# One layer pair of a hybrid decoder: the order of work in the SSD scans, in the turn to the output projection and at the entry of the FFN

## The chip, the cores and the metric

The kernel runs on one core of a Trainium2 chip. The metric is the device time of one execution in microseconds (us). TensorE is called PE here, VectorE DVE, ScalarE ACT, GpSimd POOL, and SyncE SP; SP issues nearly all DMAs.

## What is computed

The reference is a decoder trunk in float32 with 1024 tokens of width 1024 and two layers. Layer 0 is windowed attention beside a pooling mixer, then a SwiGLU FFN. Layer 1, where the change works, is a Mamba-2 SSD mixer and a second FFN:

```python
h = rmsnorm(x, mix_norm_w[1])
proj = h @ w_in                      # z (2048), xbc (3072), dt (32 heads)
xbc = silu(causal_depthwise_conv(xbc))
y = ssd_chunked(xs, dt, A, B, C) + xs * D      # 8 chunks of 128 tokens, 4 groups of 8 heads
y = y * silu(z)
y = y * rsqrt(mean(y * y over the group's 512 channels) + eps) * norm_w
x = x + y @ w_out                    # 2048 x 1024
h = rmsnorm(x, ffn_norm_w[1]); x = x + (silu(h @ w_gate) * (h @ w_up)) @ w_down
out = rmsnorm(x, final_norm_w)
```

In a chunk the scan computes C·B, masks it with the decay between tokens, multiplies it with x·dt (the diagonal part), adds C times the state before the chunk (the offset part), and updates the state.

## The kernel before

Each engine has a program of its own, written out by hand, and waits on semaphores; the order inside an engine is the order of the code. All products are three matmuls in a reduced float format: a value v is split into `hi` (rounded) and `lo` (v - hi, "the rest"), and hi·hi, lo·hi and hi·lo are added. So every operand needs an ACT instruction for `hi` and a DVE or POOL instruction for `lo`. The large products (both FFNs, the conv columns, the output projection) are done with seven instead of eight block products, M1 to M7, whose operands are sums and differences of the blocks (S1 to S4 are those of the left operand, T1 to T4 those of the FFN's input).

**Scans** (1181 to 1503 us of the trace). Four groups g of eight chunks c. Per chunk PE does `token_major` of the *next* chunk (C·B and transposes, line 2864 to 2871), the state product (L2957), the offset product (L2964), the diagonal product (L2974), and then half blocks of the z columns by `z_half` (L2228 to 2230), 12 matmuls each, 16 per group; `Z_AFTER_CHUNK` says which stand behind which chunk. ACT makes the decays (`mdec`, L2166 and L2171) and silu of z (`silu_z`). DVE masks the decays (`masked_decay`, L3835), reads the products back (`token_major`, L3768 to 3777: causal mask, B transposed, x·dt), updates the state (L3876) and writes y (L3884 to 3894). POOL scales x·dt for the state (`xds`, L1426) and the old state (L1429).

Around this run three side jobs, each of one group behind or ahead. (1) The z weights of a group are four pieces of 128x1024; SP loads them into two raw buffers, ACT makes hi (`next_hi`), POOL lo (L1143, one instruction a piece). (2) A group's y is finished in two halves of 512 tokens, h = 0 and 1, half number n = 2g + h: `gated` (times silu z, L3791), squares on ACT (L2121), their sum over four blocks on POOL (`square_sum`, L1405, three additions), a sum over partitions on PE (`square_sums`, L2883), root on ACT (L2128), reciprocal on DVE (L3796), then `root_row` on SP: the row is stored to DRAM and loaded back spread over all partitions (L939, L945). Then `row_normed` multiplies (L3802) and `mix` makes S1 to S4 (L3821). (3) SP stores the blocks to DRAM (`store_block`, L954, `gated_y`) for the projection, and loads the conv rows of the next group (`load_bc`, L885, `load_xrows`, L890) into buffers that the group before last has left.

SP works through all of that in one queue. `load_decay` (L933), first in every chunk, waits for a diagonal product, and everything behind it waits too.

**Turn and projection.** The output projection has 56 slices, (j, p): j is the block product in the order M1, M2, M5, M6, M4, M7, M3, p = 0 to 7 the 256 rows of y that it reads; p = 6 and 7 are the last group's. `OUT_SEQ` is their order, `o_places` their buffers, a ring of five behind four early ones. SP loads a slice (`load_out`, L983 and L986), ACT splits hi (`out_hi`, L2135 and L2138), DVE makes sums (`out_sum`) and the weights' rest (`out_low`, L3747), POOL the rest of y (`out_lo`, L1397), PE multiplies (`out_slice`, L2905, L2909, L2913; for p = 7 through `mm3`, L2228 to 2230) into four banks, and DVE adds the four tiles of a finished j to x (`add_result`, L3761). `out_loads` is SP's order for this part; the residual x comes back by `load_x_back`.

**Entry of the second FFN.** While the last slices (M3) run, the finished tiles of x (tt = 0 to 3 need M7, 4 to 7 need M3) are squared on ACT, normed on DVE (`make`, L3044), turned on PE (`second_T`, L2251), split on ACT and DVE (`lo`, L3101; `tail_...`, L3120 to 3157), and the first products of the FFN (L2525) wait for them: M6 for the rests of T2 (L3151).

## Time and profile before

| | us |
|---|---|
| median of 3 runs | 2369.83 (2365.24 to 2371.79) |
| the profiled execution | 2368.59 |
| its span, first to last instruction | 2366.9 |
| mean granted clock of PE | 0.982 |

The page gives busy time per engine, the chain of work that ended last, and groups of instructions. PE is busy for 96% of the span, DVE for 60%, ACT for 48%, POOL for 58%; 84% of the chain that ended last is PE. A wait is the idle time of an engine before an instruction, put down to what released it. The granted clock is PE's clock as a share of 2.4 GHz; 0.5 is its lower level, 1.2 GHz.

### The profile page before, as it was taken

The page shows a single profiled execution, that of the slowest core. Times are in us where ns is not written, and L with a number is a line of the kernel's source. Part 1 is how long each engine was busy: PE and PEld are TensorE (multiplying, and loading weights), DVE is VectorE, ACT ScalarE, POOL GpSimd, SP SyncE. Part 2 cuts the span into 40 slices and gives each one's busy share as a digit, 9 for nine tenths or more (in the row PEclk, how much of TensorE's full clock was granted, in tenths as well). Part 3 has the DMA queues.
Part 4 walks back from the last instruction along what each step waited for, and adds up shares of the span by engine and source line. Part 5 has one row for each costly group of instructions (what it writes and reads, how often), then busy time and mean ns, then how long its engine had stood idle before and what let it go on. Part 6 is the DMA issues. An engine that isn't in the chain of part 4 may idle for free.

```text
span 2366.9 us, 29286 instructions
## 1 busy us (share of the span) xinstructions
PE 2267.5 (96%) x10602; PEld 1841.8 (78%) x10602; DVE 1425.3 (60%) x1828; ACT 1146.5 (48%) x2101; POOL 1373.0 (58%) x992
## 2 busy tenths in 40 slices
PE   8999999999999999999999889779979999999998
PEld 6876888888888878888777667558768888888887
DVE  7366754333346888745578778658873424335787
ACT  4056643333334447555588767424643333333445
POOL 3234288777765654877344434235568777774654
PEclk9999999999999999999999989889999999999999
DMA  5110233232339653333444534476323233227844
GB/s 158 54 27 19 107 99 119 85 116 85 116 111 329 206 163 116 107 107 117 137 134 134 179 133 143 165 251 187 126 73 121 98 116 116 85 98 248 268 150 157
DMA packets 193787, 317.16 MB, mean 134 GB/s; under 512 B 21696, under 2 KB 106604, under 8 KB 191084
## 3 DMA queue, kind: packets, MB, share of 16 engines
q1 hardware_dynamic: 191212, 307.55, 38.6%
q10 hardware_dynamic: 2432, 7.73, 0.8%
q8 instruction: 86, 1.41, 0.2%
q14 instruction: 57, 0.47, 0.1%
HBM read 230.68 MB, written 84.56 MB: 133 GB/s over the span
## 4 chain that ended last, share of the span: by engine, by line
PE 84%; DVE 7%; DMA 3%; issue 2%; POOL 2%; SPq 1%; ACT 1%; DVEq 0%; ACTq 0%; POOLq 0%
PE ps L2525 42%; PE ps L2228 5%; PE ps L2230 5%; PE ps L2229 5%; PE ps L2617 5%; PE ps L2621 5%; PE ps L2613 5%; PE ps L2909 1%; PE ps L2913 1%; PE ps L2905 1%; PE ps L2251 1%; PE ps L2974 1%; PE ps L2694 1%; DMA bc_rows<-conv_rows 1%; PE ps L2957 1%
## 5 line engine op out<-in xcount | busy, mean ns | idle before, releaser
L1274 POOL TENSOR_TENSOR s_lo<-s_val,s_hi 128x512 fp32r<-128x512 f32 x154 | 236.1, 1539 | 197.3 <-ACT s_hi L1863 196.7
L3279 DVE TENSOR_TENSOR xres<-ps,xres 128x512 f32<-128x512 f32 x132 | 90.6, 688 | 407.5 <-PE ps L2525 407.5
L1172 POOL TENSOR_TENSOR p_lo<-p_val,p_hi 128x512 fp32r<-128x512 f32 x176 | 240.1, 1374 | 48.8 <-ACT p_hi L1616 43.3
L1616 ACT ACTIVATE p_hi<-p_val 128x512 fp32r<-128x512 f32 x176 | 111.0, 632 | 310.8 <-POOL p_val L1202 310.8
L1143 POOL TENSOR_TENSOR w_lo<-w_raw,w_hi 128x1024 fp32r<-128x1024 f32 x34 | 81.5, 2401 | 195.4 <-ACT w_hi L1471 108.7
L2525 PE MATMUL ps<-xn_hi,p_hi 128*128 128x512 f32 x704 | 190.8, 393 | 1.9 <-ACT xres L1765 1.3
L2525 PE MATMUL ps<-xn_lo,p_hi 128*128 128x512 f32 x704 | 188.8, 390 | 1.4 <-DVE xn_lo L3145 1.4
L2525 PE MATMUL ps<-xn_hi,p_lo 128*128 128x512 f32 x704 | 188.2, 389 | 0.0
L1863 ACT ACTIVATE s_hi<-s_val 128x512 fp32r<-128x512 f32 x154 | 96.9, 629 | 149.1 <-DMA d_val<-in_w_down 86.9
L2228 PE MATMUL ps<-xn_hi,w_hi 128*128 128x512 f32 x400 | 162.1, 405 | 0.0
L2229 PE MATMUL ps<-xn_lo,w_hi 128*128 128x512 f32 x400 | 157.2, 393 | 0.0
L2230 PE MATMUL ps<-xn_hi,w_lo 128*128 128x512 f32 x400 | 156.7, 392 | 0.0
L2525 PEld LDWEIGHTS ps<-xn_hi,p_hi 128*128 128x128 f32 x704 | 132.6, 189 | 30.2 <-ACT p_hi L1616 3.1
L2525 PEld LDWEIGHTS ps<-xn_lo,p_hi 128*128 128x128 f32 x704 | 132.7, 189 | 29.6 <-DVE xn_lo L3145 1.8
L2525 PEld LDWEIGHTS ps<-xn_hi,p_lo 128*128 128x128 f32 x704 | 132.1, 188 | 27.6
L2617 PE MATMUL ps<-d_lo,s_hi 128*128 128x512 f32 x560 | 151.4, 390 | 2.1 <-DVE d_lo L3331 1.9
L1397 POOL TENSOR_TENSOR os_lo<-os_val,os_hi 128x512 fp32r<-128x512 f32 x56 | 89.7, 1608 | 106.9 <-ACT os_hi L2135 106.7
L2613 PE MATMUL ps<-d_hi,s_hi 128*128 128x512 f32 x560 | 151.1, 390 | 0.0
L2621 PE MATMUL ps<-d_hi,s_lo 128*128 128x512 f32 x560 | 150.8, 389 | 0.0
L3331 DVE TENSOR_TENSOR d_lo<-rows_v,d_hi 128x512 fp32r<-128x512 f32 x108 | 127.2, 1181 | 20.9 <-ACT d_hi L1866 20.9
L1765 ACT ACTIVATE xres<-ps 128x512 f32<-128x512 f32 x132 | 77.9, 592 | 119.7 <-PE ps L2525 119.7
L2617 PEld LDWEIGHTS ps<-d_lo,s_hi 128*128 128x128 f32 x560 | 104.7, 188 | 26.1 <-DVE d_lo L3331 4.6
(385 smaller groups left out, 5680.0 us busy)
## 6 DMA issues: line engine op xcount, KB each, us to landing
s_val<-hidden SPq DMA_DIRECT2D x154, 256.0 KB, 2.9
hidden<-xres SPq DMA_DIRECT2D x20, 1792.0 KB, 6.5
wv_g<-in_w_gate SPq DMA_DIRECT2D x22, 1024.0 KB, 5.2
wv_u<-in_w_up SPq DMA_DIRECT2D x20, 1024.0 KB, 5.2
d_val<-in_w_down SPq DMA_DIRECT2D x70, 256.0 KB, 4.0
rows_v<-in_w_down SPq DMA_DIRECT2D x64, 256.0 KB, 3.7
mdec<-decay_sums SPq DMA_DIRECT2D x32, 512.0 KB, 3.9
os_val<-gated_y SPq DMA_DIRECT2D x56, 256.0 KB, 2.8
```

The costliest lines, as they stand in the source:

```text
L1172: pool.tensor_tensor(p_lo[n][:, :, :], src, f(p_hi[n][:, :, :]), ALU.subtract).then_inc(p_lo_done, 1)
L1274: pool.tensor_tensor(s_lo[i][:, :], s_val[i][:, :], f(s_hi[i][:, :]), ALU.subtract)\
L1616: act.activation(p_hi[n][:, :, :], src, ACT.Copy).then_inc(p_hi_done, 1)
L1863: act.activation(s_hi[i][:, :], s_val[i][:, :], ACT.Copy).then_inc(s_hi_done, 1)
L2228: pe.matmul(dst, l_hi, r_hi, start=first, stop=False, skip_group_check=reopened)
L2229: pe.matmul(dst, l_hi, r_lo, start=False, stop=False, skip_group_check=reopened)
L2230: return pe.matmul(dst, l_lo, r_hi, start=False, stop=last, skip_group_check=reopened)
L2525: ins = pe.matmul(bank, l_[:, k, :], r_[:, k, :], start=first and k == 0, stop=last and k == H2 - 1, skip_group_check=reopened)
L2613: pe.matmul(banks[t_], s_hi[i][:, t_ * P:(t_ + 1) * P], d_hi[i][:, :], start=p == 0, stop=False)
L2617: pe.matmul(banks[t_], s_hi[i][:, t_ * P:(t_ + 1) * P], d_lo[i][:, :], start=False, stop=False)
L2621: pe.matmul(banks[t_], s_lo[i][:, t_ * P:(t_ + 1) * P], d_hi[i][:, :], start=False, stop=False)\
L3331: dve.tensor_tensor(d_lo[i][:, :], down_operand(DOWN[j], p, i), f(d_hi[i][:, :]), ALU.subtract).then_inc(d_lo_done, 1)
```

## The change

Eight things are moved or exchanged; nothing is computed otherwise.

1. SP: in group g the rows of half 0 for group g + 1 are loaded at chunks 4 and 5 (before: 6), those of half 1 at chunk 0 of their own group (before: 7 of the one before); stores and weight pieces are spread over the chunks; the first root row of a group is sent at chunk 7 of that group (before: 0 of the next), the second at chunk 3 (before: 4).
2. DVE: norm, gating, mixes and reciprocals stand between `masked_decay(c)` and `token_major(c + 1)`, not behind it, and one or two chunks earlier.
3. The sums of squares go from POOL (three in a row) to DVE (`square_adds`, two and one); PE's sum over partitions comes at chunks 2 and 6 (before: 3 and 7), ahead of the z half blocks.
4. POOL makes the rests of the weight pieces in halves (`half_lo`), the first one ahead of `xds`.
5. ACT: squares, roots, hi of the pieces and silu change their chunks.
6. Projection: two more M2 slices stand before (0, 6) and (0, 7); slices 2, 4 and 5 are loaded at chunk 6, slice 3 at chunk 7; the order of SP in `out_loads` is new; buffers of slices 2 and 3 are other ones.
7. The rests of y for slices 0 to 15 are made by DVE (`out_s_low`), for the others by POOL as before; M1's additions come as 4 and 12 behind slices 14 and 15 (before: 8, and 4 per slice).
8. Entry of the FFN: M7's additions and squares go to p = 0 to 3, turnings to p = 1, 3, 4, 5, turning 5 ahead of the second product, and the tail's order on DVE and ACT is new.

```diff
-        OUT_SEQ = ([(0, p) for p in range(6)] + [(1, p) for p in range(3)] + [(0, p) for p in (6, 7)] ...
+        OUT_SEQ = ([(0, p) for p in range(6)] + [(1, p) for p in range(5)] + [(0, p) for p in (6, 7)] ...
...
-        SILU_AFTER_CHUNK = [{1: (0, 1), 4: (2, 3, 4)}] + [{2: (0, 1), 4: (2, 3), 6: (4, 5)}] * (G - 1)
-        NEXT_PIECE = {6: 0, 7: 1}
-        LATE_PIECE = {0: 2, 1: 3}
+        SILU_AFTER_CHUNK = [{1: (0, 1), 3: (2, 3), 5: (4,), 7: (5,)}]
+        SILU_AFTER_CHUNK += [{3: (0, 1), 5: (2, 3), 7: (4, 5)}] * (G - 2) + [{3: (0, 1), 5: (2, 3), 6: (4,), 7: (5,)}]
+        PIECE_HI = [{0: 2, 1: 3}] + [{0: 1, 1: 2, 2: 3}] * (G - 1)
+        LO_AHEAD = [{1: (2, 0), 2: (3, 0)}] + [{0: (0, 1), 1: (1, 0), 2: (2, 0), 3: (3, 0), 4: (3, 1)}] * (G - 1)
+        LO_BEHIND = [{1: (2, 1), 2: (3, 1)}] + [{1: (1, 1), 2: (2, 1)}] * (G - 1)
+        S_LO_DVE = 16
...
@@ SP, ssd_group, q = g - 1
                     if c == 0 and g:
-                        root_row(2 * g - 2)
+                        sp.wait_ge(y_stored, 16 * 14 * q)
+                        load_xrows(g, 1)
+                        sp.wait_ge(y_normed, BG * (2 * q + 1))
+                        store_blocks(q, "M4")
+                        load_piece(g, 3)
                     if c == 2 and g:
-                        first_stores(g - 1)
+                        sp.wait_ge(mix_ready, 8 * q + 2)
+                        store_blocks(q, "M5")
+                        if not last:
+                            load_piece(g + 1, 0)
+                    if c == 3 and g:
+                        sp.wait_ge(y_stored, 16 * (14 * q + 4))
+                        root_row(2 * q + 1)
-                    if c == 4 and g:
-                        sp.wait_ge(y_stored, 16 * (14 * (g - 1) + 4))
-                        root_row(2 * g - 1)
+                    if c == 4:
+                        if g and not last:
+                            load_bc(g + 1, 0)
+                        if g:
+                            sp.wait_ge(y_normed, BG * 2 * g)
+                            store_blocks(q, "M1")
+                        if g and not last:
+                            load_piece(g + 1, 1)
+                    if c == 5:
+                        if g:
+                            sp.wait_ge(mix_ready, 8 * q + 4)
...
+                        if not last:
+                            load_xrows(g + 1, 0)
+                        if g:
+                            store_blocks(q, "M7")
-                    if c == 6:
-                        if g:
-                            sp.wait_ge(y_normed, BG * 2 * g)
-                            store_blocks(g - 1, "M1", "M2")
-                            sp.wait_ge(mix_ready, 8 * (g - 1) + 4)
-                            store_blocks(g - 1, "M7")
...
-                        if not last:
-                            load_xrows(g + 1, 0)
-                            load_bc(g + 1, 0)
+                    if c == 6 and last:
+                        load_out(2)
+                        load_out(4)
+                        load_out(5)
                     if c == 7:
+                        root_row(2 * g)
+                        if not last:
+                            load_bc(g + 1, 1)
+                            load_piece(g + 1, 2)
...
+                        if last:
+                            load_out(3)
@@ SP, out_loads
+                load_out(6)
+                load_out(7)
+                load_out(8)
+                sp.wait_ge(y_stored, 16 * 14 * q)
+                root_row(2 * q + 1)
+                sp.wait_ge(y_normed, BG * (2 * q + 1))
+                store_blocks(q, "M4")
+                load_out(9)
+                sp.wait_ge(mix_ready, 8 * q + 2)
+                store_blocks(q, "M5")
+                load_out(10)
+                sp.wait_ge(y_normed, BG * (2 * q + 1) + 2)
+                store_blocks(q, "M1")
+                sp.wait_ge(y_stored, 16 * (14 * q + 6))
+                load_out(11)
...
+                sp.wait_ge(mix_ready, 8 * G)
+                store_blocks(q, "M6", "M3")
+                sp.wait_ge(y_stored, 16 * 14 * G)
+                load_out(14)
@@ POOL
+            def half_lo(piece, half):
+                cols = slice(half * BANK, (half + 1) * BANK)
+                pool.wait_ge(hi_done, piece.count(1))
+                ins = pool.tensor_tensor(w_lo[piece.slot][:, cols], raw[piece.raw][:, cols], f(w_hi[piece.slot][:, cols]),
+                                         ALU.subtract)
+                if half:
+                    ins.then_inc(lo_done, 1)
@@ DVE, ssd_group
                     masked_decay(c)
+                    if c == 0 and g:
+                        for b in range(BG):
+                            row_normed(g - 1, b, 0)
+                    if c == 1 and g:
+                        gated(g - 1, 1)
+                    if c == 2 and g:
+                        square_adds(2 * g - 1)
+                        mixes(g - 1, "S1")
+                    if c == 3 and g:
+                        reciprocal_rms(2 * g - 1)
+                    if c == 4 and g:
+                        for b in H1_ORDER:
+                            row_normed(g - 1, b, 1)
+                    if c == 5:
+                        if g:
+                            mixes(g - 1, "S3")
+                        gated(g, 0)
+                    if c == 6:
+                        square_adds(2 * g)
+                        if g:
+                            mixes(g - 1, "S2")
+                    if c == 7:
+                        reciprocal_rms(2 * g)
+                        if g:
+                            mixes(g - 1, "S4")
                     if k + 1 < NT * G:
                         token_major(k + 1)
-                    if c == 0 and g:
-                        gated(g - 1, 1)
-                        reciprocal_rms(2 * g - 2)
...
+            def square_adds(n):
+                dve.wait_ge(sq_ready, BG * (n + 1))
+                dve.tensor_tensor(sq[0][:, :], sq[0][:, :], sq[1][:, :], ALU.add).then_inc(sq_added, 1)
+                dve.tensor_tensor(sq[2][:, :], sq[2][:, :], sq[3][:, :], ALU.add).then_inc(sq_added, 1)
+                dve.wait_ge(sq_added, 2 * (n + 1))
+                dve.tensor_tensor(sq[0][:, :], sq[0][:, :], sq[2][:, :], ALU.add).then_inc(sq_summed, 1)
@@ DVE, entry of the FFN, s_ from 10
+                        if s_ < S_LO_DVE:
+                            out_s_low(s_)
-                        if (j, p) == (1, 7):
-                            quota, limit = 8, "M1"
-                        elif j >= 2 and p in (0, 1):
-                            quota, limit = (4, "M1") if j == 2 else (0, "M1")
+                        if (j, p) in ((1, 6), (1, 7)):
+                            quota, limit = 4 if p == 6 else 12, "M1"
...
+                    make(6)
+                    tail(0)
+                    make(7)
+                    tail(1)
+                    tail(2)
...
```

## Rows read from the trace of the kernel before

**Rows 1.** The page, busy time of each engine over the span.

```profile
PE 2267.5 (96%) x10602; PEld 1841.8 (78%) x10602; DVE 1425.3 (60%) x1828; ACT 1146.5 (48%) x2101; POOL 1373.0 (58%) x992
```

**Rows 2.** Windows by stage: length, then busy us (x instructions) of each engine.

```profile
1181.70:1503.50 321.80, 291.14 (x1762) 231.96 (x1761) 256.12 (x441) 240.53 (x478) 122.23 (x87) 0.95 0.42 141
1503.50:1594.00 90.50, 59.78 (x213) 45.16 (x212) 51.53 (x73) 25.26 (x44) 35.29 (x22) 0.79 0.67 235
1594.00:1676.20 82.20, 82.20 (x363) 67.72 (x363) 67.82 (x84) 38.65 (x71) 42.32 (x28) 1.00 0.57 179
1676.20:1745.30 69.10, 52.53 (x246) 41.84 (x245) 58.80 (x70) 44.36 (x86) 34.58 (x22) 0.94 0.27 95
```

**Rows 3.** Waits of PE in the scans: us in total, times, longest.

```profile
PE ps L2864 <- DMA bc_rows<-conv_rows: 20.2, 3, 7.4
PE ps L2974 <- DVE mdec L3835: 8.7, 5, 2.1
```

**Rows 4.** Timeline of PE (start us, us, instruction): three chunk starts.

```profile
1446.46 0.38 PE L2864 MATMUL ps<-bc_rows 128*128 128x128 f32 x2
...
1455.67 0.38 PE L2864 MATMUL ps<-bc_rows 128*128 128x128 f32 x2
...
1466.11 0.38 PE L2864 MATMUL ps<-bc_rows 128*128 128x128 f32 x2
```

**Rows 5.** Timeline of SP's queue: the stores and loads before a group change.

```profile
1403.47 1.79 SPq L954 DMA_DIRECT2D gated_y<-yx  x4
...
1406.92 0.68 SPq L885 DMA_DIRECT2D bc_rows<-conv_rows  x1
```

**Rows 6.** Timeline of POOL: three sums of squares.

```profile
1349.92 4.41 POOL L1405 TENSOR_TENSOR sq<-sq,sq 128x512 f32<-128x512 f32 x3
```

**Rows 7.** Timeline of DVE: masking under those sums, and without them.

```profile
1353.11 3.22 DVE L3835 TENSOR_TENSOR mdec<-mdec,cbm 128x512 f32<-128x512 f32 x2
...
1371.04 1.29 DVE L3835 TENSOR_TENSOR mdec<-mdec,cbm 128x512 f32<-128x512 f32 x2
```

**Rows 8.** Groups of DVE, 1181.7:1413.6: count, busy us, mean ns, idle before.

```profile
L3791 DVE TENSOR_TENSOR yx<-zs,yx 128x512 f32<-128x512 f32 x19 | 17.6, 983 | 0.0
L3802 DVE SCALAR_TENSOR_TENSOR yx<-yx,gconst,rr 128x512 f32<-128x512 f32 x16 | 16.7, 1106 | 0.0
...
L3768 DVE TENSOR_TENSOR cbm<-ps,tri 128x128 f32<-128x128 f32 x22 | 6.3, 285 | 28.6 <-PE ps L2866 22.6 <-PE ps L2864 6.0
```

**Rows 9.** Waits of PE, 1503.5 to 1594 us.

```profile
PE ps L2909 <- DVE od_lo L3747: 18.0, 2, 9.5
PE ps L2905 <- DVE xres L3761: 7.4, 3, 3.1
```

**Rows 10.** Timeline of DVE: gating of the last half group.

```profile
1507.94 2.50 DVE L3791 TENSOR_TENSOR yx<-zs,yx 128x512 f32<-128x512 f32 x4
```

**Rows 11.** Timeline of ACT: root of its sum of squares.

```profile
1524.36 0.36 ACT L2128 ACTIVATE rinv<-ps,eps 4x128 f32<-4x128 f32 x1
```

**Rows 12.** Chain of waits after the scan: start us, us, what.

```profile
1516.18 6.82 DMA rr_rows<-rinv
1523.02 3.93 DMA rr<-rr_rows
...
1534.11 4.41 DMA gated_y<-mix_S
1538.54 1.16 DMA rr_rows<-rinv
1539.71 3.63 DMA rr<-rr_rows
```

**Rows 13.** DMA from 1500 to 1600 us.

```profile
DMA packets 12332, 22.98 MB, mean 230 GB/s; under 512 B 1260, under 2 KB 1268, under 8 KB 12327
```

**Rows 14.** Waits of PE, 1676.2 to 1745.3 us.

```profile
PE ps L2525 <- DVE comb_lo L3151: 7.2, 1, 7.2
PE ps L2251 <- DVE xn_lo L3135: 4.1, 1, 4.1
```

More of the change, by code:

```diff
@@ L1065, in out_loads @@
+                        if last:
+                            load_out(3)
             def out_loads(load_gate):
[L1066 to L1068 removed]
+                q = G - 1
                 load_out(6)
                 load_out(7)
[L1071 to L1075 removed]
@@ L1099, in out_loads @@
+                load_out(15)
+                load_x_back(3)
+                load_x_back(7)
+                for s_ in range(16, OUTS):
                     load_out(s_)
@@ L1421, in factor @@
                         return gconst[:, g, first + c * HG:first + (c + 1) * HG].unsqueeze(2).to_broadcast([P, HG, PH])
+                    if c in LO_AHEAD[g]:
+                        b, half = LO_AHEAD[g][c]
+                        pool.wait_ge(cb_full, NT * g + c + 1)
+                        if (g, c) == (0, 1):
+                            pool.wait_ge(product_full, q_order.count(0, NQ - 1, "M4g"))
+                        half_lo(piece(b), half)
+                    if c == NT - 1 and g < G - 1:
+                        pool.wait_ge(cb_full, NT * g + c + 1)
+                        half_lo(in_group(g + 1)(0), 0)
                     if c < NT - 1:
@@ L1703, in second_entry @@
                 def second_entry():
-                    for s_ in range(5, OUTS):
+                    for s_ in range(6, OUTS):
                         j, p = OUT_SEQ[s_]
@@ L1714, in second_entry @@
                             half_square(p + 2, 0)
+                        if j == 6 and p < 4:
+                            for tt in ((0,), (1,), (2,), (3,))[p]:
+                                act.wait_ge(out_added, o_add_order.count(0, "M7", tt, 0, 1))
+                                square(tt, junk[:, :])
                         if (j, p) == (6, 2):
@@ L2182, in ssd_group @@
                         row_silu(row_at(NQ - 1, "g", 2))
-                    if c == 1 and g:
-                        squares(2 * g - 1)
-                    if c == 5:
-                        squares(2 * g)
-                    if c in LATE_PIECE:
-                        next_hi(g, LATE_PIECE[c])
-                    if c in NEXT_PIECE and not last:
-                        next_hi(g + 1, NEXT_PIECE[c])
+                    if c == 3 and g:
+                        root(2 * g - 1)
+                    if c == 7:
+                        root(2 * g)
                     if c >= 6 and last:
@@ L2934, in ssd_group @@
             def ssd_group(g):
-                last = g == G - 1
-                SUMS_AT = (3, 6) if last else (3, 7)
                 if g == 0:
@@ L2976, in ssd_group @@
                     ins.then_inc(ydiag_full, 1)
-                    if c in SUMS_AT:
-                        *first, final = Z_AFTER_CHUNK[g][c]
-                        for i in first:
-                            z_half(g, i)
-                        if c == 3 and g:
-                            square_sums(2 * g - 1)
-                        elif c == (6 if last else 7):
-                            square_sums(2 * g)
-                        z_half(g, final)
-                    else:
-                        for i in Z_AFTER_CHUNK[g][c]:
-                            z_half(g, i)
+                    if c == 2 and g:
+                        square_sums(2 * g - 1)
+                    elif c == 6:
+                        square_sums(2 * g)
+                    for i in Z_AFTER_CHUNK[g][c]:
+                        z_half(g, i)
                 t.add("chunk", NT)
@@ L3216, in second_entry @@
                     taken = 0
-                    for s_ in range(6, OUTS):
+                    for s_ in range(10, OUTS):
                         j, p = OUT_SEQ[s_]
@@ L3250, in second_entry, with tail @@
                         add_result("M3", t_, 4, 1)
-                    for q in range(4, NT):
-                        make(q)
-                    for i in range(4):
+                    make(4)
+                    make(5)
+                    def tail(i):
                         tail_t1(i)
@@ L3791, in gated, with mixes @@
                     dve.tensor_tensor(half_of(g, b, h), z[:, :], half_of(g, b, h), ALU.mult).then_inc(z_gated, 1)
+            def square_adds(n):
[4 more added lines that the diff above has]
+                dve.tensor_tensor(sq[0][:, :], sq[0][:, :], sq[2][:, :], ALU.add).then_inc(sq_summed, 1)
+            def mixes(g, *names):
+                for name in names:
+                    for i in range(2):
+                        mix(g, name, i)
             def reciprocal_rms(n):
```

269 lines of the change are left out of this document (123 added, 146 removed), and 2 rows, old and new, of the table Z_AFTER_CHUNK.

## The prediction

> **What bounds the kernel now.** I read the busy times first [rows 1]: PE works for 96% of the span, so only time in which PE waits, or multiplies at the lower of its two clock levels (1.2 instead of 2.4 GHz), can be given back. Then the windows [rows 2], cut where the diff works: the scans, the turn from scans to projection, the steady projection, the entry of the second FFN. The reader is to compare length and PE busy. The projection from 1594 us is full (82.2 of 82.2, clock 1.00) and can give nothing. In the scans PE is idle for 321.8 - 291.1 = 30.7 us, in the turn for 90.5 - 59.8 = 30.7 us, at the entry for 69.1 - 52.5 = 16.6 us, and in all three the granted clock falls below 1 (0.95, 0.79, 0.94): each longer wait is followed by some matmuls at half rate. Third the waits of PE in each stretch [rows 3, 9, 14], last the chain of waits behind the scans [rows 12].
>
> What would each stretch need at full rate? A slice of the projection is 12 matmuls: 82.2 / 363 x 12 = 2.72 us [rows 2]. A half block of z (one `z_half`) has the same 12. A chunk with two of them takes 1455.67 - 1446.46 = 9.21 us, so its own work is 9.21 - 5.44 = 3.77; one with the sum of squares takes 10.44, so that costs 1.23 [rows 4].
> - Scans: 59 half blocks (160.5) + 31 chunks (116.9) + 7 sums (8.6); at the ends of groups six products are missing, about a quarter of 3.77 each (-5.7, an estimate). Together 280.3 of 321.8: 41.5 us are lost, 30.7 idle and 10.8 at half clock.
> - Turn, first slice at 1503.5 to the start of the 18th at 1594: 17 x 2.72 + 1.23 = 47.5 of 90.5, 43 lost.
> - Entry: 16.6 idle and at most (1 - 0.94) x 69.1 = 4.1 at half clock: 20 lost.
>
> So about 105 us are there to be had, and that is the ceiling.
>
> **The change part by part.**
>
> *Loads before a group change.* Now SP issues the next group's rows at chunk 6, behind four waits and eight stores (1403.47, then the load at 1406.92 [rows 5]); PE comes to the next group's first chunk before they land and waits 20.2 us in three places, up to 7.4 each [rows 3]. In the new order rows of half 0 go out at chunk 4 or 5, behind the norm of the second half (DVE, now chunk 4) and the S3 mixes (chunk 5). From chunk 5's product to the next group's first product PE has a chunk and two half blocks and more, some 12 us, against 7.4 plus the issue. All 20.2 goes, and with it its part of the 10.8. Half 1 is loaded at chunk 0 of its own group and needed at chunk 3 or 4, over 25 us later. SP now waits in one more place, for the round trip of the root at chunk 7 and chunk 3; behind it stand the decay load of the next chunk and a weight piece. That trip's first part took 1.16 to 6.82 us [rows 12]; decay loads have two chunks, 18 us. I cost it at nothing; without that cover it is up to 5 us per group, 15.
>
> *DVE: norm, gating and mixes ahead of `token_major`.* They stand now where DVE waits for PE anyway (the idle time ahead of L3768, 28.6 us over 22 chunks [rows 8]); before, they stood between `token_major` and the masking on which the next product waits, which gave PE's 8.7 us [rows 3]. The number of these instructions is unchanged. What is new on DVE are the square sums: 3 per half group, 7 in the scans, at 1.29 / 2 = 0.65 each [rows 7]: +13.7 us. What goes is POOL's version: 4.41 us for three [rows 6], under which DVE's masking took 3.22 instead of 1.29 [rows 7], so at least 1.93 x 7 = 13.5 us less on DVE. DVE stays near 256 us busy [rows 2], of 290 instead of 322: 88%. Chunks with the heavy extras (four norms or gates at 0.98 to 1.11 [rows 8], 4.4 us) fit PE's 9.2 only because light ones follow. I keep 10 of the 41.5 us as lost. Ends: none lost (gain 41.5); or 15 behind the queue above and 10 behind DVE (gain 16). I take 31.5, nearer the first, because the largest row (20.2) is a DMA that simply goes out 12 us earlier.
>
> *POOL: rests of weight pieces in halves.* Same arithmetic, one instruction more per piece, 12 to 14 in all, on an engine busy 122 of 322 us [rows 2]. A half goes ahead of `xds` instead of a whole after it; it can delay `xds` by half of what it did. Zero, between -2 and +3.
>
> *The turn.* Today the second and third of PE's waits, 18.0 us, are for DVE rests behind the norm [rows 9]. Their chain has two round trips of the root through memory in a row: 6.82 + 3.93, then a store of 4.41, then 1.16 + 3.63 [rows 12]. The first trip now happens inside chunk 7. Slices 2, 4 and 5 load at chunk 6, which removes the wait at the third slice. Two more slices of M2 (p = 3, 4) stand before the first that needs the last group's M1 block, slice 11. PE gets to it at 11 x 2.72 + 1.23 = 31 us after the scan. Its data: gating starts at +4.5, root 12 to 16 later (1507.94 to 1524.36, of which part was the wait for the first trip [rows 10, 11]), trip 4.8 to 10.8, two norms 2.2 [rows 8], store 4.4, load as long, hi and lo rest 2: +34 to +44, middle 39. So about 8 us of waiting stay at slice 11 (3 to 13). Slice 14 loads after all stores of the last group, and slice 16 needs the 16 additions of M1, which DVE now makes in one row behind slice 14 (0.65 each, 10 us beside 8 us of PE work): 3 us each. Sum lost 14 of 43, gain 29. Ends: 3 lost (gain 40), and gain 5 if the chain takes its long values at each step and every load waits behind it in SP's order. Low rests of slices 0 to 15 move to DVE: 16 x 0.65 = 10 us, in a stretch where DVE works 51.5 of 90.5 [rows 2]; hidden, except the two ahead of the square sums.
>
> *Entry of the FFN.* M7 is added tile by tile from p = 0, turnings and the tail go up. The 4.1 us ahead of turning 6 were DVE's rest of tile 0, which moves ahead of `make(7)`: 0.5 stays. The 7.2 us [rows 14] were eight T4 and T2-rest instructions behind everything else; with two DVE instructions taken out ahead of them and turning 5 a slice earlier, I keep 3. Against that ACT now waits once per slice for DVE's addition and DVE for ACT's split; the first four slices may lose 3 where they lost 3. Gain 8, between 1 and 13.
>
> **Sum.** 31.5 + 29 + 8 = 68.5 us. The profiled execution took 2368.6 (span 2366.9 and 1.7 around it), which gives 2300; the median of the runs is 2369.8, 1.2 higher, so I say 2301.
>
> **Rivals.**
> - *The turn stays late.* SP's queue and the DMA engines take over the wait: 22.98 MB went out in 100 us, at 230 GB/s [rows 13], and must now go in about 71. If the chain to slice 11 ends at +44 and the loads behind it bunch, the turn gives 10, the scans 28, the entry 6: 44 us, 2326. For it speaks that the root's first trip took 6.82 us just where loads were queued [rows 12]; against it, that the mean hides empty stretches.
>   The Trainium skill (DMA: Bandwidth & Descriptors, "Where 436 GB/s comes from") puts one core's share of the memory at about 358 GB/s. By that the 22.98 MB need 64 us: no bar to my 71, but a bar to the next rival, whose turn would leave 60. The trace's mean of 230 neither reaches nor contradicts it.
> - *Nearly all goes.* 38 in the scans, 38 in the turn, 12 at the entry: 88 us, 2282. For it: every wait named has its cause moved. Against: the chain to slice 11 is longer than the work before it even at middle values.
> - *Slower: DVE becomes the bound of the scans.* Place: groups 1 to 3, where the norm and gating now stand ahead of `token_major`, so that every microsecond DVE is late reaches the next chunk's states. If all 90 extra instructions and 48 maskings run at the slow 3.22 / 2 = 1.61 instead of some 0.8 [rows 7], DVE needs 138 x 0.8 = 110 us more, 366 in place of 256; the scans take 366 instead of 322, +44, the other two give back 37, together +7: 2377. It decides from 322 + 37 = 359 us of DVE in the scans, 11.2 a chunk (now 8.0). Against it: POOL has 30 us less to do, and that is what slows these instructions.
> - *It doesn't bring what it says*: the waits only change their names, 2345 to 2370.
>
> **How the numbers follow.** Forecast 0.52; turn stays late 0.27; nearly all goes 0.13; slower 0.03; names change 0.05, of which 0.02 within 0.3%. A change of under 0.3%, 7 us, can't be told from none. Faster 0.95, same 0.02, slower 0.03. Range: 2282 (nearly all) to 2332 (the late turn with 6 us of POOL's and SP's bounds on top). The forecast's own range is 2288 to 2314.
>
> **What would show it.** PE's wait at L2864 for conv_rows gone; waits on masking under 5 us; scans 285 to 296 us long; DVE busy there 250 to 262. One root trip after the last scan product; PE's longest wait in the turn between 3 and 13 us at the slice (0, 6), 17 slices in 57 to 66 us. Largest wait at the entry under 4. I am wrong in the sum if DVE's busy time in the scans passes 275, if a wait for decay sums or for `xds` appears at PE's chunk starts, or if slices 3 to 10 wait for loads.

## The result, and the profile after

The changed kernel takes 2337.58 us (median of 4 runs, 2335.96 to 2337.85), the kernel before beside it 2367.53: a ratio of 0.9871 (95% interval 0.9852 to 0.989). It is faster by 30 us. The forecast of 2301 was too low by 37, and the range, which ended at 2332, missed the time.

Page of the changed kernel, busy times; then its windows, cut at the same landmarks as [rows 2] (first product of the scans, first slice, 18th slice, product of slice (5, 7), M3g).

```profile
PE 2259.0 (97%) x10602; PEld 1837.1 (79%) x10602; DVE 1409.0 (60%) x1868; ACT 1152.3 (49%) x2106; POOL 1312.3 (56%) x966
```

```profile
1180.60:1479.84 299.24, 284.94 (x1762) 228.23 (x1761) 249.62 (x469) 245.84 (x482) 91.27 (x79) 0.98 0.47 154
1479.84:1556.49 76.65, 57.55 (x215) 44.67 (x214) 48.00 (x80) 23.98 (x42) 3.90 (x3) 0.84 0.78 269
1556.49:1638.10 81.61, 81.61 (x362) 67.57 (x360) 67.79 (x87) 39.73 (x72) 49.44 (x31) 1.00 0.57 181
1638.10:1713.74 75.64, 55.06 (x246) 42.79 (x244) 60.75 (x74) 45.12 (x88) 31.71 (x21) 0.89 0.24 87
```

Set against [rows 2], the scans lost 22.6 us (forecast 31.5), the turn 13.9 (forecast 29), the steady part 0.6, and the entry got 6.5 us *longer* (forecast 8 shorter). The span fell by 32.7; of what the four windows leave, 1.1 lies ahead of the scans and 1.1 behind the start of M3g. PE did the same work: what moved is idle time and half clock.

Waits of PE in the changed kernel (us in total, times, longest), in the scans, which answer to [rows 3]; in the turn, which answer to [rows 9]; and at the entry, which answer to [rows 14]:

```profile
PE ps L2913 <- DVE btok L3810: 6.4, 3, 3.0
PE ps L3002 <- DVE mdec L3890: 5.8, 4, 3.1
PE ps L2913 <- DVE cbm L3806: 1.3, 2, 1.0
```

```profile
PE ps L2935 <- ACT od_hi L2168: 11.4, 3, 4.8
PE ps L2259 <- DVE os_lo L3785: 5.6, 1, 5.6
PE ps L2935 <- DVE xres L3799: 1.4, 1, 1.4
```

```profile
PE ps L2556 <- ACT comb_hi L1686: 12.7, 1, 12.7
PE ps L2935 <- ACT od_hi L2168: 5.6, 3, 3.2
```

No line of the first list existed before except the masking. The wait for `conv_rows` (20.2 us) is gone; in its place PE waits at its sum over partitions (L2913, `square_sums`), which the change put one chunk earlier. In the turn the rests behind the norm (18.0 us) are gone, and slices 3, 13, 14 and 15 wait for their data. At the entry one wait of 12.7 us stands where 7.2 and 4.1 stood.

### The profile page after: what moved, and what is told of

The parts are those of the page before. It is cut to its first block, busy times and chain, and to the rows that moved or that the text cites. A ratio compares the mean times of both kernels' runs of the same rounds, so it can differ in the third digit from the quotient of the medians.

```text
span 2334.2 us, 29295 instructions
## 1 busy us (share of the span) xinstructions
PE 2259.0 (97%) x10602; PEld 1837.1 (79%) x10602; DVE 1409.0 (60%) x1868; ACT 1152.3 (49%) x2106; POOL 1312.3 (56%) x966
## 4 chain that ended last, share of the span: by engine, by line
PE 84%; DVE 7%; DMA 3%; ACT 2%; issue 2%; POOL 1%; SPq 1%; DVEq 0%; ACTq 0%; POOLq 0%
PE ps L2556 43%; PE ps L2259 5%; PE ps L2261 5%; PE ps L2260 5%; PE ps L2648 5%; PE ps L2652 5%; PE ps L2644 5%; PE ps L2939 1%; PE ps L2935 1%; PE ps L2943 1%; PE ps L2725 1%; PE ps L2282 1%; PE ps L3002 1%; DVE yx L3954 1%; DVE d_lo L3364 1%
## 5 line engine op out<-in xcount | busy, mean ns | idle before, releaser
L2556 PE MATMUL ps<-xn_hi,p_hi 128*128 128x512 f32 x704 | 189.9, 392 | 14.0 <-ACT comb_hi L1686 12.7
L2648 PE MATMUL ps<-d_lo,s_hi 128*128 128x512 f32 x560 | 151.4, 390 | 1.9 <-DVE d_lo L3364 1.7
L1430 POOL TENSOR_TENSOR os_lo<-os_val,os_hi 128x512 fp32r<-128x512 f32 x40 | 63.3, 1585 | 141.5 <-DVE os_lo L3785 85.9
L2652 PEld LDWEIGHTS ps<-d_hi,s_lo 128*128 128x128 f32 x560 | 105.1, 188 | 21.9
```

Source lines behind the costliest of these rows:

```text
L2556: ins = pe.matmul(bank, l_[:, k, :], r_[:, k, :], start=first and k == 0, stop=last and k == H2 - 1, skip_group_check=reopened)
L2648: pe.matmul(banks[t_], s_hi[i][:, t_ * P:(t_ + 1) * P], d_lo[i][:, :], start=False, stop=False)
L2652: pe.matmul(banks[t_], s_lo[i][:, t_ * P:(t_ + 1) * P], d_hi[i][:, :], start=False, stop=False)\
```

## Experiments

Each run was timed in five rounds beside the kernel before. "Against the change" compares the median with 2337.6; the ratio is to the kernel before.

| run | median us | ratio (95%) | against the change |
|---|---|---|---|
| e1 tail order | 2331.7 | 0.9840 (0.9826 to 0.9855) | -5.9 |
| e2 sums later | 2325.5 | 0.9817 (0.9803 to 0.9832) | -12.1 |
| e3 slice 3's load first | 2334.3 | 0.9853 (0.9836 to 0.9869) | -3.3 |
| e4 store order | 2329.5 | 0.9833 (0.9819 to 0.9848) | -8.1 |
| e5 additions early | 2334.2 | 0.9855 (0.9842 to 0.9869) | -3.4 |
| e6 norm later | 2334.6 | 0.9862 (0.9847 to 0.9877) | -3.0 |
| e7 kernel before, rows early | 2353.0 | 0.9944 (0.9932 to 0.9957) | (-14.2 against before) |
| e8 e1 to e5 together | 2313.8 | 0.9773 (0.9760 to 0.9787) | -23.8 |
| e9 turn ordered anew | 2310.1 | 0.9757 (0.9741 to 0.9774) | -27.4 |
| e10 e9 and e6 | 2305.5 | 0.9734 (0.9718 to 0.9750) | -32.0 |
| e11 e10, stores first | 2304.4 | 0.9734 (0.9719 to 0.9749) | -33.2 |

The intervals of e3, e5 and e6 overlap that of the change and that of e1 touches it, so there the traces carry the verdict. As a yardstick for stretches whose code is the same: in the changed kernel, e1, e3, e4 and e5 the scans took 299.1 to 300.4 us from the first diagonal product to the first slice, and in the changed kernel, e1, e2 and e6 turn and steady part took 166.5 to 168.3.

### The entry: e1

```
 tail_t1(3)
 tail_t2(3)
+tail_t3(3)
+tail_b22(3)
 tail_lo1(2)
 ...
     tail_lo2(i)
-tail_t3(3)
-tail_b22(3)
```

> The changed kernel with one edit: VectorE's last difference and rest of tile 7 (tail_t3(3), tail_b22(3)) stand right behind tail_t2(3) again, ahead of the four tail_t4/tail_lo2 pairs. The changed kernel takes 2337.6 us. Theory A (the 12.70 us wait of the first M5g product at 1705.72 is the wait for tile 7's PSUM banks, read last by those two operations at 1704.35 and 1704.95): they end near 1695.4, M5g starts near 1695.6, and its sixth wait partner, M6g's pass over the low parts, is late instead, since the four pairs still end near 1705.6: entry shorter by 6 to 8 us, time 2329 to 2332. Theory B (M5g waits for ScalarE's high parts, as the page's releaser says, which come no earlier): no gain, 2336 to 2339.

Timeline of VectorE in the changed kernel (start us, us, line), and the product that waits, on TensorE:

```profile
1701.01 1.75 DVE L3163 TENSOR_TENSOR t_val<-t_val,comb_val 128x512 f32<-128x512 f32 x1
1702.68 1.74 DVE L3174 TENSOR_TENSOR comb_lo<-comb_val,comb_hi 128x512 fp32r<-128x512 f32 x1
1704.35 0.68 DVE L3153 TENSOR_TENSOR comb_val<-ps,comb_val 128x512 f32<-128x512 f32 x1
1704.95 0.67 DVE L3158 TENSOR_TENSOR xn_lo<-ps,xn_hi 128x512 fp32r<-128x512 f32 x1
```

```profile
1705.72 2.04 PE L2556 MATMUL ps<-xn_hi,p_hi 128*128 128x512 f32 x4 [12.70 <-ACT comb_hi L1686]
```

Waits at the entry in e1:

```profile
PE ps L2556 <- DVE comb_lo L3174: 5.0, 1, 5.0
PE ps L2556 <- DVE xn_lo L3158: 2.4, 1, 2.4
```

The time fell by 5.9 us, at the edge of theory A (6 to 8). L3153 and L3158 are the last two readers of tile 7's PSUM banks; M5g opens a sum in them, through `turn_free(1, 7)`. With both back in their place the wait is 2.4 us, and now carries the name of the true releaser. The page had named ScalarE's high part: it was the last event before the start, not the cause. In e1 the product starts at 1695.76, before ScalarE's first such instruction (1698.39). M6g waits 5.0 us for the last T2 rest, where it waited 7.2 in the kernel before.

### The scans: e2, e6, e7

e2, TensorE, chunk 2 of scans 1 to 3:

```
-if c == 2 and g:
-    square_sums(2 * g - 1)
 for i in Z_AFTER_CHUNK[g][c]:
     z_half(g, i)
+    if c == 2 and g and i == 4:
+        square_sums(2 * g - 1)
```

> The changed kernel with one edit: TensorE takes the sum over partitions of the odd squares (square_sums(2g-1)) after the first of the two z halves of chunk 2 instead of ahead of both. Theory A (that sum waits 6.4 us in three scans for VectorE, which stands behind square_adds and the two S1 mixes before it frees the bank, and TensorE runs at half clock after each): the 5.5 us half covers the wait, 6 to 9 us less, time 2329 to 2332. Theory B (VectorE is what paces the scans and the wait only moves to the masking or to the root): less than 2 us, 2335.5 to 2338.

First what the sum waits for, in the changed kernel. VectorE's timeline, and TensorE's:

```profile
1341.23 0.68 DVE L3834 TENSOR_TENSOR sq<-sq,sq 128x512 f32<-128x512 f32 x1
1341.83 0.68 DVE L3835 TENSOR_TENSOR sq<-sq,sq 128x512 f32<-128x512 f32 x1
1342.55 1.64 DVE L3837 TENSOR_TENSOR sq<-sq,sq 128x512 f32<-128x512 f32 x1
1344.11 1.28 DVE L3876 TENSOR_TENSOR mix_S<-yx 128x512 f32<-128x512 f32 x2
1345.31 0.28 DVE L3806 TENSOR_TENSOR cbm<-ps,tri 128x128 f32<-128x128 f32 x1
1345.51 0.27 DVE L3810 COPY btok<-ps 128x128 f32<-128x128 f32 x1
```

```profile
1345.93 1.86 PE L2913 MATMUL ps<-sq,pick 128*4 128x128 f32 x8 [2.99 <-DVE btok L3810]
1347.73 0.80 PE L2259 MATMUL ps<-xn_hi,w_hi 128*128 128x512 f32 x1
1348.32 0.63 PE L2260 MATMUL ps<-xn_lo,w_hi 128*128 128x512 f32 x1
```

The squares' sum is ready at 1344.2, but it goes into the bank that `token_major(3)` has to free, and that stands on VectorE behind the three additions and the two mixes. TensorE had been idle since 1342.9: some 1.3 us of the wait are the additions, the other 1.7 the mixes and the reading of the bank. The eight small matmuls then take 1.86 us instead of 1.03, and the z half behind them starts slow too (0.6 to 0.8 us for each of its first matmuls instead of 0.39). Window of the scans in e2:

```profile
1181.23:1468.49 287.26, 279.89 (x1761) 223.80 (x1761) 249.22 (x469) 246.26 (x483) 92.53 (x79) 1.00 0.50 160
```

12.0 us less than 299.24: 6.9 of idle time and 5.1 of half clock (PE busy 284.94 to 279.89). Theory A, and more than it promised (6 to 9): its upper end left only 2.6 us for half clock beside the 6.4 of waiting.

e6, VectorE:

```
-if c == 0 and g: row_normed(g - 1, b, 0) for the four b
-if c == 1 and g: gated(g - 1, 1)
+if c == 1 and g: the four row_normed, then gated(g - 1, 1)
```

> The changed kernel with one edit on VectorE: the four norms of the first half stand behind the masking of chunk 1 instead of behind that of chunk 0. Theory A (the 5.8 us that TensorE waits for the masking come from the 4.43 us that VectorE waits, ahead of these norms, for the root's row): the waits of 3.08 and some 0.8 us go, 3 to 7 us less than 2337.6, 2330 to 2334.5. Theory B (SyncE waits for these norms before it goes on to a weight piece and the decay loads, on which ScalarE waits 28.6 us already): the later norms make these loads later and the wait comes back, 2336 to 2345.

Waits of VectorE and of ScalarE in the scans of the changed kernel, and waits of TensorE in e6 as its timeline shows them in scan 1:

```profile
DVE yx L3853 <- DMA rr<-rr_rows: 23.0, 6, 4.4
```

```profile
ACT eacs L2189 <- DMA mdec<-decay_sums: 24.5, 9, 5.4
```

```profile
1259.62 1.10 PE L3002 MATMUL ps<-mdec,xdt 128*64 128x128 f32 x16 [0.26 <-DVE mdec L3890]
1264.19 1.13 PE L2913 MATMUL ps<-sq,pick 128*4 128x128 f32 x8 [3.48 <-DVE btok L3810]
```

The scans are 1.7 us shorter (297.58 from first product to first slice, 1.5 below the shortest of the yardstick), the median 3.0, just outside theory A's range. The mask wait of 3.08 us in scan 1 became 0.26, but the sum's wait of 0.35 became 3.48. Theory A by direction, with most of its gain turned into the other wait. VectorE stands still for 23.0 us in six places until the root's row is back from memory, where it did so nowhere in the scans of the kernel before. Only a part of that reaches TensorE: all its waits for the masking are 5.8 us. ScalarE waits 24.5 us for decay sums (before: 7.4), which SyncE issues in the same queue; whether the trip causes these was not tried.

e7, the kernel before, SyncE:

```
+c == 4, g in (1, 2): load_bc(g + 1, 0)
+(g, c) == (0, 5): load_bc(1, 0); load_xrows(1, 0)
 c == 6: sp.wait_ge(y_normed, ...)
-        store_blocks(g - 1, "M1", "M2")
         sp.wait_ge(mix_ready, ...)
-        store_blocks(g - 1, "M7"); load_xrows(g + 1, 0); load_bc(g + 1, 0)
+        load_xrows(g + 1, 0); store_blocks(g - 1, "M1", "M2", "M7")
```

> The kernel before (2368.3 us) with one edit on SyncE: the next group's B and C rows of half 0 are loaded at chunk 4, its x rows at chunk 6 ahead of the six stores instead of behind them (both at chunk 5 in the first scan). VectorE and GpSimd work as before. Theory A (the scans' gain is the wait for these rows and nothing else of the change; x rows can go out only 3 us earlier in scans 1 and 2): the 20.2 us become 3 to 8, with their half clock 14 to 21 us less, 2347 to 2354: most of the 22.6 us that the scans gained. Theory B (half of the gain is VectorE's order and GpSimd's share taken off it): the wait moves to the masking or to xds, under 9 us less, over 2359.

Window of its scans, and the two waits that stay:

```profile
1181.00:1489.50 308.50, 288.38 (x1761) 229.69 (x1760) 256.93 (x441) 240.29 (x478) 122.17 (x87) 0.97 0.45 147
```

```profile
1313.46 0.79 PE L2866 MATMUL ps<-bc_rows 128*128 128x128 f32 x2 [4.57 <-DMA yx<-conv_rows]
...
1400.13 0.80 PE L2866 MATMUL ps<-bc_rows 128*128 128x128 f32 x2 [4.54 <-DMA yx<-conv_rows]
```

Earlier rows alone, with VectorE and GpSimd untouched, took 13.3 us off the scans [rows 2], for 11.1 us less of waiting (20.2 to 9.1): theory A by the time, with a little more wait left than its 3 to 8. By the same rate the 9.1 us that stay are worth about 11 (an estimate from these two figures), which makes some 24 in all, 1.6 more than the 22.6 that the scans gained. By that estimate everything else in the scans (VectorE's order, the squares moved off GpSimd, against the new wait) cost 1.6 net, and with e2's 12.0 for the wait it brought some 10 of its own. No run tried that part alone, so the 10 are not shown.

### The turn: e3, e4, e5

e3, SyncE, chunk 7 of the last scan:

```
+if last: sp.wait_ge(mix_ready, 8 * g); load_out(3)
 root_row(2 * g)
 ...
 store_blocks(q, "M3")
-if last: load_out(3)
```

> The changed kernel with one edit: SyncE issues the loads of output slice 3 ahead of the last root row's store, wait and load and of the M3 stores, 6 us earlier (near 1481 instead of 1486.8). Theory A (the turn is late by SyncE's order, in a chain: slice 3's wait of 4.84 us also holds ScalarE, behind it the last root, behind that all stores of the last scan and the loads of slices 13 to 15): the 4.84 us go and the later stores come 5 to 7 us earlier, 7 to 14 us less in all, time 2323 to 2331. Theory B (the transfers at 1530 to 1550, at some 400 GB/s, set the end of the turn whatever came before): the 4.84 us come back at slices 13 to 17, 0 to 3 us less, 2334.5 to 2338.

SyncE's queue in the changed kernel, from the root's row to slice 3's loads, and the slice on TensorE; then the reciprocal on VectorE that the root's row waits for, and SyncE's longest single wait between 1440 and 1482 us:

```profile
1480.77 0.33 SPq L946 DMA_DIRECT2D rr_rows<-rinv  x1
1485.45 0.32 SPq L952 DMA_DIRECT2D rr<-rr_rows  x1
1485.87 0.85 SPq L961 DMA_DIRECT2D gated_y<-mix_S  x2
1486.77 0.45 SPq L987 DMA_DIRECT2D os_val<-gated_y  x1
```

```profile
1494.11 2.04 PE L2935 MATMUL ps<-od_hi,os_hi 128*128 128x512 f32 x4 [4.84 <-ACT od_hi L2168]
```

```profile
1473.60 0.94 DVE L3847 RECIPROCAL rinv<-rinv 4x128 f32<-4x128 f32 x1 [1.55 <-ACT rinv L2158]
```

```profile
SPq L987 <- PE ps L2261: 11.6, 1, 11.6
```

The queue is late before the root's row already. `load_out(2)`, which the change puts at chunk 6, waits for the last z half block, and SyncE stands there for 11.6 us, until 1478.02. The reciprocal is done at 1474.54, but its row goes out at 1480.77, behind the six loads of slices 2, 4 and 5, and slice 3 behind the row's trip. What it would bring to send the row ahead of `load_out(2)` was not tried; e3 moves slice 3 alone.

In e3 that wait is gone. These are there, at slices 8, 10, 13 and 14; the last two stood before as well, with 2.60 and 3.95:

```profile
1504.91 1.20 PE L2940 MATMUL ps<-od_lo,os_hi 128*128 128x512 f32 x4 [1.10 <-DVE od_lo L3781]
1512.82 1.21 PE L2940 MATMUL ps<-od_lo,os_hi 128*128 128x512 f32 x4 [2.08 <-DVE od_lo L3781]
...
1524.58 1.25 PE L2936 MATMUL ps<-od_hi,os_hi 128*128 128x512 f32 x4 [3.45 <-ACT od_hi L2169]
1533.43 2.05 PE L2936 MATMUL ps<-od_hi,os_hi 128*128 128x512 f32 x4 [4.28 <-ACT od_hi L2169]
```

From the first slice to the first turning (all of turn and steady part) it takes 167.4 us, in the changed kernel 167.0: nothing gained in the turn; the 3.3 us of the median lie within the intervals. Theory B by the size. But the trace gives another reason than the transfers at 1530 to 1550: the root came 5.2 us earlier (its row is stored at 1493.55, not 1498.76), and then lost 3.1 of them, since the trip took 4.31 us behind the loads of slices 6 to 8 instead of 1.18. What comes last is the last scan's stores, and they came only 2.3 us earlier.

e4, SyncE:

```
 load_out(8)
+for tt in (4, 0, 5, 1): load_x_back(tt)
 ...
 store_blocks(q, "M2")
-load_x_back(0); load_x_back(4); ... store_blocks(q, "M7"); load_out(13)
-load_x_back(1); load_x_back(5); ... store_blocks(q, "M6", "M3")
-sp.wait_ge(y_stored, 16 * 14 * G); load_out(14); ... load_out(15); ...
+load_out(13); sp.wait_ge(y_stored, 16 * (14 * q + 8)); load_out(14); load_out(15)
+... store_blocks(q, "M7"); load_out(16); ... store_blocks(q, "M6", "M3")
+load_x_back(2); load_x_back(6); load_out(17); load_x_back(3); load_x_back(7)
+(the wait for all stores ahead of load_out(22))
```

> The changed kernel with SyncE's order in the turn changed: four of the eight 512 KB loads of parked rows are issued at 1491, in the idle stretch of the DMA engines, the loads of slices 14 and 15 wait for the M2 stores alone and are issued ahead of the M7, M6 and M3 stores, the wait for all stores stands ahead of slice 22. Theory A (slices 13 to 17 wait because their loads stand behind stores and parked rows that nobody needs yet): 3.95 us at slice 14, 5.59 at 15 and most of 2.60 at 13 go with their half clock, 8 to 13 us less, time 2324 to 2330. Theory B (bandwidth: the same bytes are to be moved before slice 18 at up to 400 GB/s): the waits move to slices 6 to 13 or 16 to 20, 0 to 3 us less, 2334.5 to 2338. Loads of the parked rows beside slices 6 to 8 and the last root's row could also cost up to 3 us.

Turn and steady part take 160.3 us instead of 167.0, the median falls by 8.1: theory A. The waits of 2.60 and 3.95 us at slices 13 and 14 are gone. Two rows show what then ends last:

```profile
1533.91 2.48 DVE L3801 TENSOR_TENSOR xres<-ps,rows_v 128x512 f32<-128x512 f32 x4 [6.91 <-DMA gated_y<-mix_S]
```

```profile
1538.26 0.80 PE L2261 MATMUL ps<-od_hi,os_hi 128*128 128x512 f32 x1 [7.60 <-DVE os_lo L3787]
```

The additions of M1 write `xres`, in which the mixes lie until they are stored, so they wait for the last scan's last stores; and slice 15's rests stand behind them on VectorE.

e5, VectorE:

```
-if s_ + 1 < OUTS: out_sum(s_ + 1)
+if s_ + 1 < OUTS and s_ != 15: out_sum(s_ + 1)
 out_low(s_); out_s_low(s_)
+if s_ == 15: four additions; out_sum(16)
-quota = 4 if p == 6 else 12
+quota = 8 if p == 6 else 4
```

> The changed kernel with one edit on VectorE: slice 15's two rests stand ahead of out_sum(16), and 8 instead of 4 of the 16 additions of M1 stand between slices 14 and 15, 4 ahead of out_sum(16) and 4 behind it. The changed kernel takes 2337.6 us. Theory A (the 5.59 us at slice 15 are VectorE's order: it waits until 1544.19 for slice 16's weights, though slice 15's high part is there at 1540.7, and the 12 additions in one row hold slice 16): slice 15 starts near 1542, slice 16 near 1549.5 instead of 1553.2, 3 to 5 us less, 2332.5 to 2335. Theory B (the stretch is paced by the transfers, and the additions need the parked rows, which land no earlier): 0 to 1.5 us less, 2336 to 2338.

```profile
1544.58 0.50 PE L2259 MATMUL ps<-od_hi,os_hi 128*128 128x512 f32 x1 [2.14 <-DVE os_lo L3790]
```

5.59 us became 2.14, turn and steady part 164.3, 2.2 below the shortest of the yardstick: theory A, at its lower end. (The first slice stands 2.1 us later in this trace than in that of the changed kernel, which the start times carry along.)

### Together: e8 to e11

> The changed kernel with the edits of the first four runs and that of the fifth together. Alone the first four gave 6, 12, 3 and 8 us against 2337.6. Theory A (each takes away a wait of its own): they add up, 29 us, and 3 of the fifth, 2303 to 2310. Theory B (the turn's edits work on the same wait, the last scan's stores, and the DMA engines at 400 GB/s bound them): only 18 of tail and sums and 6 to 8 of the turn, 2311 to 2315.

2313.8, theory B: the scans take 289.1 (e2: 287.3), the entry from its first turning to M6g's last pass 60.0 as in e1 (changed kernel 66.0), but turn and steady part 159.6, only 0.8 better than e4 alone. In e8:

```profile
1495.63 2.74 DVE L3861 SCALAR_TENSOR_TENSOR yx<-yx,gconst,rr 128x512 f32<-128x512 f32 x4 [6.90 <-DMA rr<-rr_rows]
...
1523.61 4.88 DVE L3807 TENSOR_TENSOR xres<-ps,rows_v 128x512 f32<-128x512 f32 x8 [6.67 <-DMA gated_y<-mix_S]
```

With slice 3 first, the root is ready at 1482.7, and its row (2 KB) now stands behind 2 MB of parked rows: store issued at 1484.25, load at 1492.04.

e9 is e8 with SyncE's order `load_out(7)`, `root_row(2q+1)`, `load_out(8)`, the stores, parked rows in pairs, and all stores ahead of slices 14 and 15; VectorE has 8 additions behind slice 13 and slice 15's rests ahead of the other 8. e10 adds e6.

> The kernel of the run before (all five edits, 2313.8 us), with the turn's order changed once more. There the four early parked rows stood ahead of the last root's row, whose trip took 7.8 us, and the additions of M1 waited 6.67 us for the last stores, with slice 15's rests behind them (9.34 us of TensorE at slice 15). Now the root's row goes out behind the loads of slice 7, the parked rows behind it in pairs; the M7, M6 and M3 stores go out as soon as their mixes are done, ahead of the loads of slices 14 and 15; on VectorE 8 additions stand behind slice 13, and slice 15's rests ahead of the other 8. Theory A (the order of SyncE's queue and of VectorE sets the turn): the last stores land near 1514 instead of 1523, slice 16 starts near 1527 instead of 1535, 6 to 10 us less, 2304 to 2308. Theory B (the DMA engines bound it: 21 MB at 400 GB/s are 53 us of the 65 from the first slice to the 18th): 0 to 4 us less, 2310 to 2314.

> The kernel of the run beside it, and VectorE's four norms of the first half behind the masking of chunk 1. Alone that gave 3.0 us, with the waits for the masking (5.8 to 2.9 us) partly turned into waits of the sum over partitions; here that sum is covered by a z half. Theory A: both gains stand, 3 to 6 us less than the run beside it. Theory B (VectorE has no more room in chunks 1 and 2, and the later sum delays the root): 0 to 1.5 us less or slower.

e9 gave 3.6 us against e8 (4.4 in turn and steady part, 155.1), in theory B's range by the size: the M7, M6 and M3 stores go out from 1507.1, not at 1512.5 and 1515.6. But slice 10 waits 4.57 us: its rest stands on VectorE behind the S2 mix, which waits for the M1 stores, and those stand behind 1 MB of parked rows. What holds it up there is again an order, not the rate of the transfers. e10 gave 4.6 more, theory A (scans 286.5 instead of 289.6, PE busy in them 280.16; the turn and steady part are 3.5 shorter as well, though the edit is in the scans). Windows of e10, scans, then turn and steady part together:

```profile
1181.12:1467.65 286.53, 280.16 (x1762) 223.85 (x1761) 249.33 (x469) 246.40 (x483) 89.49 (x79) 1.00 0.50 161
1467.65:1619.26 151.61, 142.06 (x611) 114.92 (x609) 129.12 (x173) 67.16 (x122) 50.74 (x34) 0.98 0.71 239
```

> The kernel of the last run (2305.5 us) with one edit: two 512 KB loads of parked rows that stood ahead of the last scan's M1 stores stand behind them. Theory A (the stores that the last mixes and slice 11 wait for are held up by what is queued ahead of them: at some 400 GB/s 1 MB is 2.6 us): VectorE's wait of 3.95 us for the M1 stores and TensorE's of 3.93 us at slice 11 shrink by 2 to 3 us, the last stores go out that much earlier, 1.5 to 3.5 us less, 2302 to 2304. Theory B (the same bytes have to go before the additions anyway, and the engines are at 400 GB/s from here on): the 2.6 us come back at slice 14, no change, 2304.5 to 2306.5.

e11 took 2304.4, turn and steady part 151.4: no change that can be told from none, so theory B, though the time lies between the two ranges. VectorE's wait for the M1 stores fell from 4.0 to 1.4 us and TensorE's of 3.93 to 1.87 (it is slice 10's, not slice 11's, as I had written), and waits of 1.57 and 0.64 us came up at slices 11 and 15, not at slice 14 as theory B had it. e10 and e11, with one ratio of 0.9734, are 32 to 33 us faster than the changed kernel and come within 5 us of the time I had forecast for it.

## Why the prediction missed

Of the signs I had named, these came: the wait for `conv_rows` gone, DVE busy 249.6 us (said: 250 to 262). These did not: masking under 5 us (5.8), scans 285 to 296 us (299.2), 17 slices in 57 to 66 us (76.7), the turn's longest wait at the slice (0, 6) (none there; 5.6 at (1, 7)), one root trip after the last scan product (two, with stores at 1480.77 and 1498.76, the last product having ended near 1479.9), largest wait at the entry under 4 (12.7). And slice 3 waited for its load, which I had named as what would make the sum wrong.

- **What bounds it: right.** The full-rate need of the scans, 280.3 us of PE, is what e2 and e10 show (279.89, 280.16 busy, clock 1.00).
- **Loads before a group change: right.** All 20.2 us went; e7 shows that the loads' place alone takes 11.1 of them away, at 1.2 us for each us of wait.
- **DVE ahead of `token_major`: the step that failed in the scans.** Busy time came as said (249.6, forecast 250 to 262). But I weighed VectorE by its busy time and took only the masking for exposed (5.8 us, said: under 5 to 10). Moved ahead of `token_major`, the additions and mixes also stand ahead of the bank that PE's sum takes. PE waited 7.7 us there, and e2 took 12.0 away, half clock included, where I had no term. Lost in the scans 18.9, kept 10; with e2's one edit 7.0 are lost. The root's trip, which "I cost ... at nothing" with a view to SyncE's queue alone, costs something by another way: VectorE waits 23.0 us for it, the longest time (4.43 us) shortly ahead of the 3.08 us masking wait, and e6, which puts the norms later, gains 1.7 us in the scans.
- **POOL in halves: right**, 0.6 us of waits for `xds`.
- **The turn: failed by 15 us.** The two root trips [rows 12] no longer stand in a row, but "the first trip now happens inside chunk 7" failed: both come after the last scan product, the first 6.2 us later than its row was ready, since the loads of slices 2, 4 and 5 ahead of it waited for the last z half block. The 8 us at slice 11 did not come: its rest began at +37 us (1517.1; my middle was +39), but PE got there at +39, not +31, held at slice 3 by 4.84 us and by the slow matmuls behind it. Slice 11's wait is hidden by that, not gone. I had taken slices 2 to 10 as loaded. Slice 3's load stood behind `root_row(2g)`: of what stands behind that trip in SyncE's queue I had named decay loads and a piece, and left slice 3 out. For slice 14, which loads after all stores, and for slice 16 with the additions I gave 3 us each; slices 13 to 15 took 12.1 idle, slice 16 another 1.4. The last stores were issued from 1520.93 and slice 14's load at 1530.54, 9.6 us later, and parked rows stood ahead of the loads of slices 13 and 15. I had priced the additions by VectorE's time and not by what they can wait for, the stores out of `xres`; in e4 that is 6.91 us. Idle was 19.1 us, half clock 10.0 (76.65 - 57.55, and 57.55 - 47.5).
- **The entry: wrong sign.** I counted "two DVE instructions taken out ahead of" the T2 rests and did not ask who waited for those two. They free M5g's banks: 12.7 us of waiting where I had kept 3, and 5.9 us less in e1. With them back the entry is as long as before, so the 8 us did not come either: M6g still waits 5.0, and the slices of the last product wait 2.24 and 3.25 us for ScalarE's high parts, which stand there among squares that wait for VectorE's additions tile by tile. I had given the slices 3 us, as before.
- **Rivals.** *The turn stays late* was nearest (2326, for turn 10, scans 28, entry 6): stores and loads bunched in SyncE's order are what e4 and e9 show. But its other condition, a chain to slice 11 that ends at +44, did not come (+37). It had a chance of 0.27; its time is 12 us short of the measured one, for which its entry term, 12.5 us off, suffices.

## What to carry to other kernels

Before moving work forward on an in-order engine, list for every instruction that it passes who waits for that one, buffers that it frees included, and put a matmul that needs another engine's latest results between pieces of independent work. A root or a flag that travels through memory belongs ahead of the bulk transfers in its queue, and ahead of whatever waits for a buffer there: the store of the same 2 KB row took 1.2 us when the loads issued before it had landed, 4.3 us behind the loads of three slices (e3) and 7.8 us behind 2 MB (e8). Price TensorE's waits together with the slow matmuls behind them: in the turn 10.0 us stood beside 19.1 of idle time, in e2 5.1 went with 6.9, in e7 2.8 with 10.5.

## What the runs showed of the hardware

DMA of the changed kernel from 1530 to 1550 us, 40 slices of half a microsecond:

```profile
GB/s 8 0 4 131 315 402 238 115 262 369 385 385 336 365 373 258 274 324 406 385 397 397 410 410 402 397 410 397 397 401 397 410 402 410 414 397 414 418 451 344
```

One core moved some 400 GB/s for 10 us on end, where the mean of [rows 13] had shown 230. The prediction had weighed a share of 358 GB/s (Trainium skill, DMA: Bandwidth & Descriptors, "Where 436 GB/s comes from"); with one core at work the trace goes past it, and the measurement decides. That bound was no bar to the rival that it was held against, whose turn would have left 60: in e11 the 17 slices take 61.0 us, with 378 GB/s on the mean from 1490 to 1530 us, and turn and steady part move the same 36 MB in 151.4 us instead of 167.0.

Behind waits of up to 1.02 us at the sum, in the changed kernel, its eight matmuls took 1.03 us and the z half behind them ran at its usual pace. Behind the waits of 2.99 and 3.02 us slow matmuls followed both times, but not the same ones: once the eight took 1.86 us, once they took 1.03 and the first nine of the z half were slow. Removing 6.9 us of idle time in e2 removed 5.1 us of slow matmuls with it, and the granted clock of the scans went from 0.98 to 1.00.
